# The last head's four value tiles move from the end of the value projection in among the score and value products of the recurrent branch

## The reference, cut to what matters

```
s   = (q . k) * w_intra          # scores times weights from the gates
num = s @ v ;  den = sum of s    # the kernel holds all 512 tokens at once: no carried state
h   = num / max(|den|, exp(-m))
```

## Time and profile before

| | |
|---|---|
| median of 3 runs | 3531.24 us (3530.91 to 3531.88) |
| time of the profiled execution | 3530.89 us |
| its span in the trace | 3529.1 us |
| TensorE busy with matmuls | 3383.2 us (96%) |
| VectorE busy | 2051.9 us (58%) |
| ScalarE busy | 662.5 us (19%) |
| chain that ended last, by engine | TensorE 90%, VectorE 6%, ScalarE 2%, DMA 1% |

### The profile page before, as it was taken

The page is one execution under the profiler, slowest core; times in us unless marked ns, Lnnn a source line. Parts: engine busy times, 40 slices in busy tenths (PEclk is TensorE's granted clock), DMA queues, the critical chain, the costliest instruction groups (busy, mean ns, idle before and its releaser), DMA issues.

```text
span 3529.1 us, 51831 instructions
## 1 busy us (share of the span) xinstructions
PE 3383.2 (96%) x21526; PEld 2966.3 (84%) x21526; DVE 2051.9 (58%) x4167; ACT 662.5 (19%) x1561; POOL 182.8 (5%) x140
## 2 busy tenths in 40 slices
PE   8999989998999989989999999999999999999998
PEld 5878645787888878868999999987899899987898
DVE  3587553464653167564897675534575766434574
ACT  2101342012221021242121111023111111033111
POOL 0000000003453300000000000000000000000000
PEclk9999999999999999999999999999999999999999
DMA  5244001222223335403445444432344444432443
GB/s 228 78 167 167 24 25 60 91 89 72 84 89 127 131 102 196 174 25 139 149 168 168 150 168 139 154 131 94 133 168 166 140 168 139 154 120 99 139 169 120
DMA packets 65609, 450.19 MB, mean 128 GB/s; under 512 B 7136, under 2 KB 10336, under 8 KB 13792
## 3 DMA queue, kind: packets, MB, share of 16 engines
q1 hardware_dynamic: 65376, 446.88, 36.6%
HBM read 445.80 MB, written 1.05 MB: 127 GB/s over the span
## 4 chain that ended last, share of the span: by engine, by line
PE 90%; DVE 6%; ACT 2%; DMA 1%; issue 1%; SPq 0%; DVEq 0%; ACTq 0%
PE bank L1174 61%; PE bank L908 14%; PE bank L1344 3%; PE bank L1426 2%; PE bank L958 2%; DVE conv_sum L2417 1%; PE bank L1028 1%; PE bank L976 1%; PE bank L1053 1%; PE bank L1468 1%; PE bank L1107 1%; PE bank L1129 1%; DMA weight_ring<-w_q 1%; PE bank L1118 0%; DVE region_b L2156 0%
## 5 line engine op out<-in xcount | busy, mean ns | idle before, releaser
L1174 PE MATMUL bank<-normed,weight_ring 128*128 128x128 f32 (+1 forms) x5472 | 765.4, 296 | 20.6 <-DVE normed L2778 9.9
L1174 PEld LDWEIGHTS bank<-normed,weight_ring 128*128 128x128 f32 x5472 | 709.6, 193 | 70.0 <-issue 36.5
L1174 PE MATMUL bank<-normed,mixer_small 128*128 128x128 f32 (+1 forms) x3040 | 385.1, 281 | 3.6 <-DVE normed L2799 3.6
L1174 PEld LDWEIGHTS bank<-normed,mixer_small 128*128 128x128 f32 x3040 | 364.4, 192 | 9.4 <-issue 4.6
L908 PE MATMUL bank<-normed,weight_ring 128*128 128x256 f32 (+1 forms) x1088 | 295.7, 422 | 0.9 <-DVE region_o L2219 0.6
L1174 PE MATMUL bank<-region_a,weight_ring 128*128 128x128 f32 (+1 forms) x2128 | 294.5, 293 | 0.6 <-DVE region_a L2372 0.6
L1174 PEld LDWEIGHTS bank<-region_a,weight_ring 128*128 128x128 f32 x2128 | 272.1, 192 | 16.7 <-issue 7.1
L908 PEld LDWEIGHTS bank<-normed,weight_ring 128*128 128x128 f32 x1088 | 200.5, 190 | 76.6 <-issue 55.2
L1174 PE MATMUL bank<-turned,weight_ring 128*128 128x256 f32 (+1 forms) x944 | 199.0, 353 | 0.0
L1174 PEld LDWEIGHTS bank<-turned,weight_ring 128*128 128x128 f32 x944 | 163.6, 190 | 18.4
L1174 PE MATMUL bank<-region_a,mixer_small 128*128 128x128 f32 (+1 forms) x1232 | 160.5, 282 | 0.0
(11 more groups left out here) (310 smaller groups left out, 4689.8 us busy)
## 6 DMA issues: line engine op xcount, KB each, us to landing
weight_ring<-w_ada SPq DMA_DIRECT2D x48, 1024.0 KB, 6.3
weight_ring<-w_up SPq DMA_DIRECT2D x44, 1024.0 KB, 4.8
weight_ring<-w_f1up SPq DMA_DIRECT2D x44, 1024.0 KB, 4.8
weight_ring<-w_f2up SPq DMA_DIRECT2D x44, 1024.0 KB, 4.8
weight_ring<-w_gt SPq DMA_DIRECT2D x32, 1024.0 KB, 4.8
weight_ring<-w_qk SPq DMA_DIRECT2D x24, 1024.0 KB, 4.9
weight_ring<-w_v SPq DMA_DIRECT2D x20, 1024.0 KB, 4.9
weight_ring<-w_pj SPq DMA_DIRECT2D x16, 1024.0 KB, 4.8
```

Of the source, the lines that this page charges most:

```text
L1174: mm = nc.tensor.matmul(bank[u.bank][:, pair.columns(p)], lhs(k), rhs(k), start=begins and p in pair.opens and k == 0, stop=ends and p in ...
```

## The change

The value projection keeps the tiles of heads 0 to 2 (n = 0 to 11). The four tiles of head 3 (n = 12 to 15) are computed inside `mlstm`: tile 12 behind `A.0.1`, tile 13 behind `A.1.0`, tile 14 behind `A.1.1`, tile 15 behind `hT.0`. ScalarE copies them at these places: 12 between the forward and the backward exponentials of head 0; 13 ahead of the forward exponentials of head 1; 14 behind these and ahead of `head_rms(0)`; 15 ahead of the forward exponentials of head 2. The mean and variance sums, and ScalarE's work that hangs on their numbers, move one tile earlier. Ahead of `pv.3.0` TensorE waits for tile 15's copy. The plan hands out the same number of banks, in the new order.

```diff
-MEAN_AT, VARIANCE_AT = 6, 9
+MEAN_AT, VARIANCE_AT = 5, 8
...
# TensorE, mlstm
                 emptied(pe, plan.pairs[f"q{l}"][-1].unit(4))
-                emptied(pe, plan.units[f"v{l}"][-1])
+                emptied(pe, plan.units[f"v{l}"][(HEADS - 1) * QT - 1])
...
                     running_max(h, 0)
                     if h >= 2:
                         turn_head(h - 2)
+                    if h in (1, 2):
+                        value_tile(l, HEADS - 1, 2 * h - 1)
                     if h:
                         weights_of(h - 1, 1)
                     running_max(h, 1)
+                    if h in (0, 1):
+                        value_tile(l, HEADS - 1, 2 * h)
+                    if h == HEADS - 1:
+                        emptied(pe, plan.units[f"v{l}"][-1])
                     weights_of(h, 0)
...
# ScalarE, mlstm, behind the copies of the scores
+                    if h in (1, 2):
+                        value_copy(l, (HEADS - 1) * QT + 2 * h - 1)
                     weights_of(h, 0)
+                    if h in (0, 1):
+                        value_copy(l, (HEADS - 1) * QT + 2 * h)
                     if h:
                         head_rms(h - 1)
                     weights_of(h, 1)
...
# ScalarE, value projection
-                for n, u in enumerate(plan.units[f"v{l}"]):
-                    full_bank(u)
-                    a_(vaug[:, n % QT, n // QT, 0:HD], bank[u.bank][:, 0:HD], ACT.Copy).then_inc(bank_free[u.bank], 1)
+                for n in range((HEADS - 1) * QT):
+                    value_copy(l, n)
                     conv_norm(l, c0, n)
```

More of the change, by code:

```diff
@@ L358, in make_plan, with value_unit @@
         plan.paired_with_chunks(f"o{l}", l, h, LATE[4:8])
-        for n in range(HEADS * QT):
+        def value_unit(n):
             if n % QT == 0:
@@ L363, in make_plan @@
             plan.blocks[f"v{l}"][-1].after = plan.units[f"v{l}"][-1]
+        for n in range((HEADS - 1) * QT):
+            value_unit(n)
             if n == MEAN_AT:
@@ L373, in make_plan @@
                 plan.take_units(f"hT{l}.{h - 2}", 2)
+            if h in (1, 2):
+                value_unit((HEADS - 1) * QT + 2 * h - 1)
             if h:
@@ L376, in make_plan @@
             plan.take_units(f"A{l}.{h}.1", 1)
+            if h in (0, 1):
+                value_unit((HEADS - 1) * QT + 2 * h)
             plan.take_units(f"pv{l}.{h}.0", nq)
@@ L1010, in chunks_after, with value_tile @@
                 return after
+            def value_tile(l, h, t):
+                u, b = plan.units[f"v{l}"][h * QT + t], plan.blocks[f"v{l}"][h]
+                if t == 0:
+                    landed(b)
+                cols = tile(b, 0, 2 * KD).rearrange("p (m k c) -> p k m c", m=2, k=KD)
+                begin(u)
+                for k in range(KD):
+                    mm = nc.tensor.matmul(bank[u.bank][:, 0:HD].rearrange("p (m c) -> p m c", m=2),
+                                          hn[:, k, t * P:(t + 1) * P], cols[:, k], start=k == 0, stop=k == KD - 1)
+                mm.then_inc(bank_full[u.bank], 1)
             def mlstm(l, full):
@@ L1335, in _ @@
                     columns(l, chunks[-1])
-                for h, b in enumerate(plan.blocks[f"v{l}"]):
-                    landed(b)
-                    cols = tile(b, 0, 2 * KD).rearrange("p (m k c) -> p k m c", m=2, k=KD)
+                for h in range(HEADS - 1):
                     for t in range(QT):
[L1341 to L1347, removed]
+                        value_tile(l, h, t)
                         if h * QT + t == MEAN_AT:
@@ L1621, in dn_squares, with value_copy @@
                 A.sent(post_sq, 2)
+            def value_copy(l, n):
+                u = plan.units[f"v{l}"][n]
+                full_bank(u)
+                a_(vaug[:, n % QT, n // QT, 0:HD], bank[u.bank][:, 0:HD], ACT.Copy).then_inc(bank_free[u.bank], 1)
             def mlstm(l, full):
```

## The result

The changed kernel takes 3520.07 us (median of 8 runs, 3516.86 to 3524.25) against 3531.07 for the kernel before, timed beside it: ratio 0.9969, 95% interval 0.996 to 0.9978, 11.0 us less (7.8 to 14.1). Forecast were 3518.2 and 13.0 less. A second timing gave 0.9974 (0.9963 to 0.9985), 9.2 less. The profiled execution took 3518.65 us; its span is 3516.9, 12.2 under before.

What follows compares the result with a forecast made beforehand. TensorE, holding 90% of the chain, was taken to bound the kernel. Gains of 6.7 us in layer 0 and 6.3 in layer 1 sum to 13.0: 3530.89 becomes 3517.9 profiled, 3518.2 as median; range 3513.5 to 3525.5.

Steps and rivals of the forecast that it cites:

- Entrance: Start of the recurrent branch: ScalarE's later SiLUs cost 0 in layer 0 and 0.7 us in layer 1.
- Tile 12 is free: TensorE's hole ahead of head 0's first products: the tile fits, with 0.17 us to spare in layer 0, cost 0.
- The clock, -1.96 a layer: First products of each layer's recurrent branch: with the wait filled the clock stays up, saving 1.96 us a layer.
- rival 1: Ahead of `pv.2.0` in layer 0, a hole grown to 2.5 us drops the clock: 1.96 us, total 3520.1; chance 0.18.
- Tile 13, +3.0 and +3.2: Between head 0's first products and `head_rms(0)`: the tile costs 3.0 us in layer 0, 3.2 in layer 1.
- tile 14, +2.1 and +2.2: `head_rms(0)` stands behind this tile's copy on ScalarE and begins 2.1 us later in layer 0, 2.2 in layer 1.
- Tile 15, +3.4 and +3.35: Head 2: first argument to gate_out takes 3.4 us longer in layer 0; exponentials come 3.35 later in layer 1.
- +0.5 for the plan's order: `pv.2.0` in layer 0: all four of its banks come free only with gate_out, so it ends some 0.5 us later.
- The mean's product: Layer 1's value projection: one tile earlier, this product still comes after the last tap, by 0.6 us; no cost.
- DMA: 0: Fourth issue of the next weights comes some 35 us later; its block serves late in attention, so cost 0.

Runs made afterwards that it cites:

- the one-tile version: The kernel before with one value tile moved behind `A.0.1` in both layers, the other 15 left in the projection: 3522.32 us, ratio 0.9969.
- the spread version: Against the change, one value tile directly ahead of each head's forward products, copies of 13 to 15 behind `head_rms`: 3507.85 us, 0.9926; again 3505.8, 0.9927.
- the later copies: The change with ScalarE's copies of tiles 13 and 15 behind their head's forward exponentials, tile 14's behind the head norm: 3516.61 us, 0.9959.
- The earlier norm: The change with the layer norm's mean and variance sums, and ScalarE's part of it, one tile earlier still: 3523.77 us, 0.9969.

## Why the prediction was right, and where not

- **Entrance.** Right. First argument in layer 0 at 369.51 - 362.41 = 7.10, as before; in layer 1 at 5.65, +0.7, released by ScalarE's copies of the scores.
- **Tile 12 is free.** Right: first products at 11.40 and 9.07; the one-tile version gains 3.45 in each layer. (Tile 12 begins at 7.59, which is what the rows gave, and not at 7.78; and half the row of 384.80 ends at 6.81, not 6.91. Nothing hangs on either.)
- **The clock, -1.96 a layer. This term failed.** I read one profile's half clock as a property of the 3.65 and 3.19 us waits. In four profiles of the same kernel each first group was slow three times, and head 3's group in layer 0, behind 2.10 us, three times too. The change took the first wait away in both layers, and the half clock turned up behind later ones: head 2's group in layer 0 slow in all three profiles (that is rival 1), layer 1's last in two of three. The credit was 3.9 us; what the seven profiles show is none: 8.9 us gained without slow groups, 8.6 with them. Over all eight profiles with a tile in the first wait, leaving out the spread version, 10 groups on the chain were slow, or 1.25 a run, against 7 in the four of before, or 1.75. At 1.69 us each that is 0.8 us less a run, so little or nothing of the credit came in. The forecast without it, 13.0 - 3.9 = 9.1, is what the profiles show. The size was off too: a slow group costs 1.69, not 1.96. The 6.29 us were read with the last matmul's tail of 0.16 and the 4.33 without it, and a group behind a wait takes 4.44 by the same count, 0.1 more than one that follows another.
- **Tile 13, +3.0 and +3.2; tile 14, +2.1 and +2.2.** Right: `head_rms` at 34.44 (34.25 worked out) and 26.95 (26.7), head 2's argument at 45.45 (45.28) and 33.90 (33.65). That the delays lie side by side is shown by the later copies.
- **Tile 15, +3.4 and +3.35; +0.5 for the plan's order.** Right: gate_out at 56.61 (56.42). Head 3's argument at 70.04 instead of 68.0 carries the slow group, 1.7, and 0.35 of small errors; in layer 1 it is at 49.59 (49.2).
- **The mean's product.** The taps end at 1454.30, TensorE arrives at 1454.99: the margin held. It is 0.7 us; the prediction counted six tiles as 20.72, where the row less a tile and its tail gives 20.81. The earlier norm shows what its loss costs.
- **DMA: 0.** The issue came 33 us later (412.46 against 379.28), as worked out, and in the waits from 456 to 670 us no engine waits for that block; the one wait for a weight block there, VectorE's for `w_ga`, is 11.2 us long in both kernels.

Without the clock, the sum was good to 0.2 us in all (9.1 against 8.9). With it the forecast was 4 us too good by the profiles. That the median came out only 2 us from the forecast, and on rival 1's 3520.1, is in part luck: its 11.0 us are 2 more than the stretches show, and its interval, 7.8 to 14.1, holds both 9 and 13. So the range was met with one term of the sum wrong.

## What to carry to other kernels

Work moved into another stage pays only for the part that falls into a wait of the engine that does it: here four tiles of 3.45 us gained 4.65 in layer 0 at the change's places, and 11.6 where each stood directly ahead of a group of forward products and the copies stood behind the head norm. Long waits on the engine that copies (up to 5.7 us on ScalarE) say little: taking three of them away in each layer gave 1.4 us in all, since TensorE's own path was nearly as long. And a half clock in one profile is to be counted as a chance at every wait of TensorE, not as a fixed cost of one; several profiles of the same kernel tell how often each group is slow.

## What the hardware showed

The same kernel, the same wait, another clock: behind 3.65 us of idle TensorE's next 20 instructions took 6.29, 4.60, 6.14 and 6.29 us in four profiles, and behind head 3's 2.10 us the next 18 took 4.17, 5.85, 5.80 and 5.85. In all eight profiles with a tile in the first wait, leaving out the spread version, some later group was slow, on the chain in six of them. The waits ahead of slow groups of products were 1.97 to 3.65 us long. The Trainium skill (TensorE: Matmul & The Clock Gate, "What's actually happening") calls the number of slow matmuls at a kernel's start run-variable; these rows show the like behind waits in the middle of one.
